# Samples' paged softmax moved from the out-projection into the end of the mixer, and the value pages multiplied in one run of sixteen matmuls

## The reference

```python
def fox_sample(q, k, v, logf, pool_k, pool_v, pool_lf, page_table):
    ...
    k_all = jnp.concatenate([pool_k[page_table].reshape(n, past, HA, DA).astype(k.dtype), k], axis=1)
    v_all = jnp.concatenate([pool_v[page_table].reshape(n, past, HA, DA).astype(v.dtype), v], axis=1)
    lf_all = jnp.concatenate([pool_lf[page_table].reshape(n, past, HA).astype(F32), logf], axis=1)
    cum = jnp.cumsum(lf_all, axis=1).transpose(0, 2, 1)
    logits = jnp.einsum('nqhd,nkhd->nhqk', q, k_all).astype(F32) * scale
    logits = logits + cum[:, :, past:, None] - cum[:, :, None, :]
    ...
    p = jax.nn.softmax(logits, axis=-1).astype(v.dtype)
    return jnp.einsum('nhqk,nkhd->nqhd', p, v_all)
```

## Time and profile before

| | |
|---|---|
| median of 3 runs | 3112.16 us (3105.6 to 3116.91) |
| time of the profiled execution | 3107.7 us |
| its span in the profile | 3105.9 us |
| PE busy | 2890.0 us, 93% |
| DVE, ACT, POOL busy | 1737.5, 1169.8, 317.9 us |
| mean granted TensorE clock | 0.945 of 2.4 GHz |

### The profile page before, as it was taken

One profiled execution on the slowest core, in us unless ns is written; L12 is line 12 of the kernel. 1 busy time (PEld: TensorE's weight loads), 2 busy tenths in 40 slices (PEclk: granted clock), 3 DMA queues, 4 the chain that ended last, 5 costly groups with the idle time before them and its releaser, 6 DMA issues. The chain is left out here.

```text
span 3105.9 us, 45239 instructions
## 1 busy us (share of the span) xinstructions
PE 2890.0 (93%) x18076; PEld 2519.8 (81%) x18076; DVE 1737.5 (56%) x2811; ACT 1169.8 (38%) x1863; POOL 317.9 (10%) x148
## 2 busy tenths in 40 slices
PE   6799999889999999999777999997999999999996
PEld 3587888778778889999736878886888788999995
DVE  1285444316676676676604944444066767676765
ACT  1232333424444445444312413334154444444442
POOL 4111100023000000000042210101230000000000
PEclk7899999969999999999867999998799999999998
DMA  8313121143333232323181211122422332332231
GB/s 333 117 34 106 43 61 47 41 132 110 95 92 92 89 100 90 91 89 95 38 341 51 92 48 49 49 69 72 139 76 89 94 96 89 95 96 89 89 96 65
DMA packets 380712, 293.37 MB, mean 94 GB/s; under 512 B 25725, under 2 KB 326309, under 8 KB 379710
## 3 DMA queue, kind: packets, MB, share of 16 engines
q1 hardware_dynamic: 376208, 288.45, 29.5%
q10 hardware_dynamic: 4302, 2.15, 0.2%
HBM read 267.68 MB, written 23.71 MB: 94 GB/s over the span
## 5 line engine op out<-in xcount | busy, mean ns | idle before, releaser
L1551 PE MATMUL tslot<-g_hi,w_hi 128*128 128x260 f32 (+1 forms) x2496 | 679.8, 326 | 10.8 <-DVE g_lo L2160 6.1
L1551 PE MATMUL tslot<-g_hi,w_lo 128*128 128x260 f32 (+1 forms) x2496 | 672.8, 324 | 0.0
L1551 PE MATMUL tslot<-g_lo,w_hi 128*128 128x260 f32 (+1 forms) x2496 | 671.0, 323 | 0.0
L1551 PEld LDWEIGHTS tslot<-g_hi,w_hi 128*128 128x128 f32 x2496 | 420.1, 191 | 53.4 <-issue 9.3
L1551 PEld LDWEIGHTS tslot<-g_hi,w_lo 128*128 128x128 f32 x2496 | 419.1, 191 | 39.4
L1551 PEld LDWEIGHTS tslot<-g_lo,w_hi 128*128 128x128 f32 x2496 | 419.1, 191 | 38.4
L1522 ACT ACTIVATE w_hi<-w_raw 128x1024 fp32r<-128x1024 f32 x292 | 307.1, 1052 | 358.3 <-PE tslot L1937 312.4
L2276 DVE TENSOR_TENSOR cat<-cat,tslot 128x512 f32<-128x512 f32 (+1 forms) x320 | 220.6, 690 | 193.7 <-PE tslot L1937 192.4
L1526 DVE TENSOR_TENSOR w_lo<-w_raw,w_hi 128x1024 fp32r<-128x1024 f32 x256 | 311.9, 1218 | 0.0
L1937 PE MATMUL tslot<-f_hi,w_hi 128*128 128x260 f32 (+1 forms) x1056 | 283.9, 323 | 6.8 <-DVE w_lo L1526 4.5
L1937 PE MATMUL tslot<-f_hi,w_lo 128*128 128x260 f32 (+1 forms) x1056 | 282.3, 322 | 0.0
(11 more groups left out here) (318 smaller groups left out, 4052.1 us busy)
## 6 DMA issues: line engine op xcount, KB each, us to landing
w_raw<-in_ffn_up_dram SPq DMA_DIRECT2D x176, 512.0 KB, 3.7
a_raw<-in_ada_w_dram SPq DMA_DIRECT2D x24, 2048.0 KB, 17.0
w_raw<-in_ffn_down_dram SPq DMA_DIRECT2D x88, 512.0 KB, 3.6
w_raw<-in_w_in_dram SPq DMA_DIRECT2D x46, 512.0 KB, 3.9
w_raw<-in_w_o_dram SPq DMA_DIRECT2D x32, 512.0 KB, 3.9
x_hold<-x_res SPq DMA_DIRECT2D x2, 4128.0 KB
x_res<-x_hold SPq DMA_DIRECT2D x2, 4128.0 KB, 12.2
x_res<-in_cache_v_dram SPq DMA_DIRECT2D x32, 256.0 KB, 3.0
```

The source lines that it names most:

```text
L1551: last = pe.matmul(out[:, at + a:at + b], w[:, kk, :], x[:, kk, t0 + a:t0 + b], start=(kk == 0 and first), stop=(kk == KD - 1 and w is w_lo))
```

## The change

Bias, rows, softmax and the turned probabilities move from tiles 0 to 5 of the out-projection into phases 38 to 42 of the mixer. Their scratch is now in mixer buffers (`sq`, `gdiag`), and their PSUM in `x_bank`. The 16 transfers of `cache_logf` move with them: they stand in SP's queue between `load(10)` and `load(11)` of the mixer. The softmax results are written over `k.lg` and `k.v_new`.

In the tail, DVE first builds `pts`, two zeroed 128 x 288 buffers with the probabilities in 4 of every 36 columns, so that a window of 32 columns at 32 s holds only sample s in its own 4 columns. The values are multiplied in the 16 matmuls of `sample_values`, now with 32 columns of `pts` as weights and 512 columns of a value page (four heads side by side) moving, all summed in one 32 x 512 PSUM region. They stand in tile 6, ahead of kk = 4. ACT copies that region to SBUF (`sample_rows` in the tail), and `sample_columns` in tile 7 picks each head's own rows with 4 matmuls. DVE's `sample_out` and `sample_low` follow after m = 6, where `sample_low` was after m = 7.

```diff
--- before.py
+++ after.py
...
+                if n == 10:
+                    sp.wait_ge(g_sq_used, 9)
+                    for i in range(S * NPG):
+                        sp.dma_start(lf[:, i // NPG, i % NPG, :], d["cache_logf"][L, bass.ds(page(i), 1)].rearrange(
+                            "o p h -> p (o h)")).then_inc(lf_loaded, 16)
...
+            def sample_bias():
+                pe.wait_ge(e_ready, 1)
+                pe.wait_ge(prod_done, 2 * HA)
+                pe.wait_ge(lf_loaded, 16 * S * NPG)
+                for pg in range(NPG):
+                    out = x_bank[:, R * pg:R * pg + R]
+                    pe.matmul(out, const(k, "after"), lf[:, :, pg, :], start=True, stop=False)
+                    for later in range(pg + 1, NPG):
+                        pe.matmul(out, ones, lf[:, :, later, :], start=False, stop=False)
+                    last = pe.matmul(out, ones, e_new, start=False, stop=True)
+                last.then_inc(b_ready, 1)
+
+            def sample_rows():
+                pe.wait_ge(lg_ready, 1)
+                pe.wait_ge(qk_ready2, 1)
...
+            def sample_probs():
+                pe.wait_ge(prob_ready, 2)
...
+                if p == 39:
+                    sample_bias()
+                if p == 40:
+                    sample_rows()
+                if p == 42:
+                    sample_probs()
...
+                if p == 41:
+                    act.wait_ge(neg_ready, 1)
+                    act.activation(rows, rows, ACT.Exp, bias=one[:, 1:2], accum_out=one[:, 2:3]).then_inc(exp_done, 1)
...
+                if p == 38:
+                    sample_terms()
+                if p == 39:
+                    sample_logits()
+                if p == 40:
+                    sample_top()
+                if p == 41:
+                    sample_normalize()
+                if p == 42:
+                    sample_turned()
...
-            for n in range(S * NPG):
-                page = sp.value_load(k.pages[0:1, n:n + 1], min_val=0, max_val=N_POOL - 1)
-                sp.dma_start(lf[:, n // NPG, n % NPG, :], d["cache_logf"][L, bass.ds(page, 1)].rearrange(
-                    "o p h -> p (o h)")).then_inc(lf_loaded, 16)
...
-            def sample_bias():
-                ones, after = const(k, "ones"), const(k, "after")
...
+            def sample_values(n):
+                if n == 0:
+                    pe.wait_ge(pt_moved, NPG)
+                    pe.wait_ge(v_loaded, 16 * S * NPG)
+                s, pg = divmod(n, NPG)
+                last = pe.matmul(slot[2][0:R, BANK:BANK + HA * DA], pts[pg][:, R * s:R * s + R], vp[:, s, pg, :], start=(n == 0),
+                                 stop=(n == S * NPG - 1))
+                if n == S * NPG - 1:
+                    last.then_inc(v_summed, 1)
+
+            def sample_columns():
+                pe.wait_ge(orow_ready, 1)
                 for h in range(HA):
-                    for s in range(S):
-                        for pg in range(NPG):
-                            last = pe.matmul(slot[2][:, BANK + S * h + s:BANK + S * h + s + 1], vp[:, s, pg, DA * h:DA * h + DA],
-                    for s in range(S):
-                        for pg in range(NPG):
-                            last = pe.matmul(slot[2][:, BANK + S * h + s:BANK + S * h + s + 1], vp[:, s, pg, DA * h:DA * h + DA],
-                                             pt[:, pg, HA * s + h:HA * s + h + 1], start=(pg == 0), stop=(pg == NPG - 1))
-                last.then_inc(v_summed, 1)
+                    last = pe.matmul(slot[2][:, S * h:S * h + S], orow[:, DA * h:DA * h + DA], ident[0:R, h:R:HA], start=True, stop=True)
+                last.then_inc(turned, 1)
...
-                    if hf == 0:
-                        step = {(1, 0): sample_bias, (2, 0): sample_rows, (4, 0): sample_probs, (5, 4): sample_values}.get((m, kk))
-                        if step:
-                            step()
+                    if (hf, m, kk) == (0, 6, 4):
+                        for n in range(S * NPG):
+                            sample_values(n)
+                    if (hf, m, kk) == (0, 7, 4):
+                        sample_columns()
...
+            def sample_rows():
+                act.wait_ge(v_summed, 1)
+                act.wait_ge(ctx_turned, 1)
+                act.activation(orow, slot[2][0:R, BANK:BANK + HA * DA], ACT.Copy).then_inc(orow_ready, 1)
...
+            def sample_probs():
+                for pg in range(NPG):
+                    dve.memset(pts[pg], 0.0).then_inc(k.zeroed, 1)
+                dve.wait_ge(k.zeroed, 2 + NPG)
+                for pg in range(NPG):
+                    dve.tensor_copy(pts[pg].rearrange("p (s x) -> p s x", s=S)[:, :, 0:HA], k.lg[:, pg, :, :]).then_inc(pt_moved, 1)
...
             lower(0)
-            sample_bias()
+            sample_probs()
             lower(1)
-            sample_logits()
             for m in range(1, KD):
                 add_square(0, m)
-                if m == 2:
-                    sample_top()
-                elif m == 3:
-                    sample_normalize()
-                elif m == 4:
-                    sample_turned()
-                elif m == 5:
+                if m == 6:
                     sample_out()
-                elif m == 7:
                     sample_low()
             dve.wait_ge(x_back, 16)
             steps = joins[0].on_dve(dve)
@@ -2296,7 +2325,7 @@
                         st.low(dve, item_of(u + 4))
                     side(i)
 
-            dve.wait_ge(k.zeroed, 2)
+            dve.wait_ge(k.zeroed, 2 + NPG)
             steps1 = joins[1].on_dve(dve)
 
             def side0(i):
```

More of the change, by code:

```diff
@@ L776, in block_mixer @@
         N_POOL = d["cache_k"].shape[1]
+        (lf_loaded, e_ready, b_ready, lg_ready, qk_ready2, rows_ready, rows_link, neg_ready, exp_done, prob_ready, pt_ready) = (
+            k.sem("p_" + n) for n in ("lf_loaded", "e_ready", "b_ready", "lg_ready", "qk_ready", "rows_ready", "rows_link", "neg_ready",
+                                      "exp_done", "prob_ready", "pt_ready"))
+        R = S * HA
+        lf = sq[0][:, 0:NPG * R].rearrange("p (s g h) -> p s g h", s=S, g=NPG)
+        e_new, qk = (sq[1][:, R * i:R * i + R].rearrange("p (s h) -> p s h", h=HA) for i in range(2))
+        rows, dnew, one = gdiag[0][0:R, 0:PAST + 1], gdiag[1][0:R, 0:R], gdiag[1][0:R, R:R + 4]
         SPREADS = {14: (0, 0), 20: (0, 1), 23: (1, 0), 29: (1, 1), 32: (2, 0), 33: (2, 1), 37: (3, 0), 38: (3, 1)}
@@ L1125, in norm_rows @@
                 last.then_inc(g_rows, 1)
+            def sample_bias():
[13 more added lines that the diff above has]
+                for pg in range(NPG):
+                    pe.matmul(x_bank[0:R, P * pg:P * pg + P], k.lg[:, pg, :, :].rearrange("p s h -> p (s h)"), ident, start=True, stop=True)
+                pe.matmul(x_bank[0:R, PAST:PAST + 1], qk.rearrange("p s h -> p (s h)"), ones[:, 0:1], start=True,
+                          stop=True).then_inc(rows_ready, 1)
+            def sample_probs():
+                pe.wait_ge(prob_ready, 2)
+                for pg in range(NPG):
+                    pe.matmul(x_bank[:, R * pg:R * pg + R], rows[:, P * pg:P * pg + P], ident[0:R, 0:R], start=True, stop=True)
+                pe.matmul(x_bank[:, 2 * R:3 * R], ones[0:R, :], dnew, start=True, stop=True).then_inc(pt_ready, 1)
             for p in range(LAST):
@@ L1826, in out_tile @@
                 half_product(pe, k, st, n, slot[n % 2], HALF_BASE[hf], hf, hook).then_inc(st.used, 1)
-            def sample_bias():
-                ones, after = const(k, "ones"), const(k, "after")
-                pe.wait_ge(e_ready, 1)
-                pe.wait_ge(lf_loaded, 16 * S * NPG)
-                for pg in range(NPG):
-                    out = slot[2][:, R * pg:R * pg + R]
-                    pe.matmul(out, after, lf[:, :, pg, :], start=True, stop=False)
-                    for later in range(pg + 1, NPG):
-                        pe.matmul(out, ones, lf[:, :, later, :], start=False, stop=False)
-                    last = pe.matmul(out, ones, e_new, start=False, stop=True)
-                last.then_inc(b_ready, 1)
@@ L1840, in sample_rows @@
-            def sample_rows():
-                pe.wait_ge(lg_ready, 1)
-                pe.wait_ge(qk_ready, 1)
-                for pg in range(NPG):
-                    pe.matmul(slot[2][0:R, BANK + P * pg:BANK + P * pg + P], k.lg[:, pg, :, :].rearrange("p s h -> p (s h)"), ident,
-                              start=True, stop=True)
-                pe.matmul(slot[2][0:R, BANK + PAST:BANK + PAST + 1], qk.rearrange("p s h -> p (s h)"), const(k, "ones")[:, 0:1], start=True,
-                          stop=True).then_inc(rows_ready, 1)
@@ L1849, in sample_probs @@
-            def sample_probs():
-                pe.wait_ge(prob_ready, 2)
-                for pg in range(NPG):
```

(20 more changed lines are left out.)

77 lines of the change are left out of this document (37 added, 40 removed).

## The result

| | before | changed |
|---|---|---|
| median, runs beside each other | 3108.88 us (3104.6 to 3116.91, 4 runs) | 3033.4 us (3030.64 to 3036.15, 4 runs) |
| profiled execution | 3107.7 us, span 3105.9 | 3034.32 us, span 3032.5 |
| mean granted clock | 0.945 | 0.961 |

The ratio is 0.9754, with a 95% interval of 0.973 to 0.9778: the kernel is 2.5% faster. The forecast of 3047 us had the sign and most of its terms right; one term, the low clock behind the context turning, was wrong, and the time lies 0.6 us under the range of 3034 to 3066.

The account below looks back on a forecast made before the run. PE, busy 2890 of 3105.9 us, bounds the kernel, with waits and low clock in the out-projection. 2 x (35.6 - 3.0) = 65.2 us off gives 3040.7 span, 3042.5 profiled, 3047 us against the median; range 3034 to 3066.

Parts of the forecast that it names:

- I keep both: Out-projection: context turning stays at 4.4 us, and the tile behind it takes 2.6 us more than an undisturbed one.
- rival D: Products take half the price, or low clock behind the context turning goes (2.6 us per layer): 3033 to 3042; 0.05.
- 2 x 35.6: Out-projection, end of tile 0 to tile 8: 61.7 us against 97.3, 35.6 us less per layer, two layers.
- the 4.5 that I added: Profiled execution lay 4.5 us under the median of the runs shown, 3112.16; this raises 3042.5 to 3047.
- The waits ahead of tiles 1, 2 and 4: Out-projection: PE's waits of 11.16, 2.06 and 2.21 us, forecast to go.
- The products: Sixteen f32 value products of 512 columns in tile 6: 13.7 us at full clock, 27.4 at 1.2 GHz.
- The columns: `sample_columns`, eight records: 1.1 us, plus 0.3 us of waiting for ACT's copy out of PSUM.
- The mixer: Mixer's end moves by 3.0 us per layer from added PE and DVE work; bounds 1.25 and 7.4.
- B: Mixer's end costs its upper bound, 7.4 us per layer: 3056, or 3066 if tile 2 waits 5 us; 0.16.
- C: Sixteen products run at 1.2 GHz and leave a spell behind: 13.7 + 2.5 us more per layer, 3079; 0.06.
- E: No gain: waits return in the mixer, PE standing for `lf` or `prob_ready` 33 us per layer: 3112; 0.02.
- F: Slower: SP's 16 transfers hold up weight tile 11, costing once they end past 500 us; up to 3222; 0.01.

Follow-up runs that it names:

- e2: Changed kernel with the values multiplied as before, in 64 one-column products at the same place in tile 6: 3058.79 us.
- e5: Changed kernel with the context turning one tile (5.6 us) earlier, behind tile 1 instead of tile 2: 3038.38 us.
- e7: Changed kernel with the samples' normalization moved into VectorE's wait for the last exponential, and the turning back one phase later: 3037.32 us.
- e9 to e12: Changed kernel with the context turning 0.7 us earlier, or 1.4, 2.8, 5.6 us later: 3036.03, 3042.97, 3040.89, 3042.28 us.
- e6: Changed kernel with `sample_low` back behind m = 7 on VectorE: 3037.0 us.
- e1: Kernel before, with only the sixteen log-forget page transfers moved into the mixer behind weight tile 10: 3073.63 us, ratio 0.9871.
- the control: Changed kernel unaltered, run again on the same chip as the others: 3036.11 us.

## Why the prediction was right or wrong, point by point

**What failed: "I keep both".** The forecast kept the context turning at 4.4 us and the 2.6 us of low clock behind it, as rows of before had them, and gave them no other bound; their going stood only in rival D, with 0.05. The changed kernel has 3.7 us (635.04 less 631.35) and 0. That is 3.3 of the 3.55 us by which the stretch from the end of tile 0 to tile 8 came out shorter (678.23 - 620.08 = 58.15 against 61.7). And it isn't that rival's reason, a missing stop, that took the cost away: 12 layers without a stop have it (e2, e5, e7, e9 to e12). The term depended on where the piece falls behind the clock's last rise; in both layers it falls into the free stretch, at 15.12 us behind the rise. That is luck: nothing in the edit aims at it, and e2 and e7, edited elsewhere, have it free in one layer and not in the other. A term of this kind needed both its prices, 3.7 and 7.0 us; the forecast of the profiled execution would then have reached 6.6 us lower, and the range with it.

**The rest of the 13.6 us between 3047 and 3033.4.** In profiled executions the difference was 3042.5 to 3034.3, 8.2 us: 7.4 less in the two stretches of tiles 0 to 8 than by the forecast of 2 x 35.6, 0.9 more in the mixers, and 1.7 less in stretches that no edit touches, within what these vary. The other 5.4 us come mostly from the 4.5 that I added because the first three runs of before had a median 4.5 above its profiled execution. Beside the changed kernel that distance was 1.2, and for the changed kernel it was -0.9.

**What held.** The waits ahead of tiles 1, 2 and 4 went, and tile 8's with them, by the earlier `sample_low` (e6). The products: 13.85 us against 13.7, so 32 columns of weights cost what 128 do. The columns: 0.99 us (675.36 - 674.37), with no visible wait for ACT's copy; 1.4 forecast. Tile 2 does not wait: ACT reads tile 0 at 622.86, 2.8 us after its end, and tile 2 is due 5.7 after it. x starts back at 668.71 and lands 13.9 us later, and PE has no wait up to 700: the join is not held. SP's transfers issue at 462.96 to 480.84, tile 11 at 480.89, ahead of the 500 us where they would have cost. SP's queue in the changed kernel:

```profile
462.96 17.88 SPq L853 DMA_DIRECT2D gsq<-in_cache_logf_dram  x16
480.89 0.43 SPq L811 DMA_DIRECT2D w_raw<-in_w_in_dram  x1
...
668.71 0.34 SPq L1868 DMA_DIRECT2D x_res<-x_hold  x1
```

**The mixer.** 3.0 us forecast, 2.9 and 3.9 in the profiled execution. Over the 26 layers of the changed kernel and of the experiments that kept its mixer the mean is 343.4 us, against 340.35 over four layers with the old one (before, e1): 3.1. Like with like, the layers with the half-clock stretch ahead of tile 0 give 343.7 against 340.8, the ones without it 341.2 against 338.9: 2.9 and 2.3. The sum held; of its parts only DVE's was shown, 0.64 us ahead of the gate (0.41 ahead of the last maximum, 0.23 behind it, where I had 0.8 and 0.45). The split of the rest between PE's small matmuls and its clock was not tried apart.

**The rivals.** B (7.4 us in the mixer) did not happen: the granted clock is 1.00 from 480 to 590 us, past the last dense pass. C, the products at half clock, is refuted by 0.87 us for each. D's second half is what happened, at 3033 where it said 3033 to 3042. E and F fail with the waits and with SP's queue.

## What to carry to other kernels

A group of small matmuls that lasts as long as this one (32 records, 3.7 us) has two prices, and which one you read in a trace depends, in these runs, on where it falls behind the clock's last rise; half a microsecond turned it over between e7 and the control, so put both into a forecast, or cut the group into pieces between large matmuls. Many one-column products belong with the wide operand moving: same sums, here 13.85 us for 24 to 25, and the clock stays up. Small transfers behind which an engine waits belong in an earlier, idle part of the queue; here they alone gave nearly half of the gain.

## What the runs showed of the hardware that I had not expected

The same 32 small matmuls, at the same distance from the start of the same tile (18.50 and 18.51 us), left the clock at 2.4 GHz in one run and took it to 1.2 GHz in another: 3.7 us and nothing behind, or 4.7 us and 11 matmuls of 0.43 us where they need 0.23. What TensorE did before was alike, except that the clock had risen 0.5 us later in tile 0 (4.02 us into it, against 3.51). Eight records at a time never did it, in 24 groups (four in each of six layers). And 128 one-column records took 23 to 25 us in the three kernels that have them, some 0.19 us each, with six to twelve half-clock matmuls behind them.
